# The last two attention units and the delta-rule scan: which goes first in each turn, and how the decay steps are spread

## The reference

```python
h = rmsnorm(x, norm1_w); proj = h @ w_in
o_a = gated_delta_rule(qa, ka, va, g, beta)          # 4 heads, chunks of 64 tokens
o_a = rmsnorm(o_a, gdn_norm_w) * silu(z)
o_b = dilated_attention(qb, kb, vb)                  # 8 heads of 64 features
x = x + concat([o_a, o_b]) @ w_out
...
def step(state, xs):                                 # inside gated_delta_rule, 8 chunks in sequence
    u = uv - wk @ state
    o = qd @ state + at @ u
    state = ge * state + ke.T @ u
```

## Time and profile before

| | us |
|---|---|
| median of 3 timed runs (1449.32 to 1449.98) | 1449.7 |
| the profiled execution | 1449.33 |
| its span, first to last instruction | 1447.5 |
| TensorE busy | 1419.6 (98%) |
| VectorE busy | 817.4 (56%) |
| ScalarE busy | 610.7 (42%) |
| GpSimd busy | 134.3 (9%) |
| decays stage (panels 141 to 143) | about 906.8 to 935 |
| panel 147 with scan and units 10 and 11 | 978.5 to 1026.5 |

### The profile page before, as it was taken

The page is one execution under the profiler, slowest core; times in us unless marked ns, Lnnn a source line. Parts: engine busy times, 40 slices in busy tenths (PEclk is TensorE's granted clock), DMA queues, the critical chain, the costliest instruction groups (busy, mean ns, idle before and its releaser), DMA issues.

```text
span 1447.5 us, 19982 instructions
## 1 busy us (share of the span) xinstructions
PE 1419.6 (98%) x7898; PEld 1134.1 (78%) x7898; DVE 817.4 (56%) x1394; ACT 610.7 (42%) x1104; POOL 134.3 (9%) x116
## 2 busy tenths in 40 slices
PE   8999999999999999999999999999999999999997
PEld 6777777788788888888877777776778888888886
DVE  4545555557674343443468767676555763664463
ACT  4544455542363231322335755344444432342234
POOL 0000000012200000000012000440020210110012
PEclk9999999999999999999999999999999999999999
DMA  7222222113223223222233221110222232222221
GB/s 254 83 82 85 87 81 73 59 59 131 88 74 116 87 102 103 87 102 89 101 106 131 88 73 59 64 42 1 103 103 85 105 106 99 90 100 102 85 66 68
DMA packets 40348, 130.92 MB, mean 90 GB/s; under 512 B 4800, under 2 KB 5184, under 8 KB 40256
## 3 DMA queue, kind: packets, MB, share of 16 engines
q1 hardware_dynamic: 39392, 128.08, 25.5%
q10 hardware_dynamic: 864, 1.57, 0.3%
HBM read 124.92 MB, written 4.19 MB: 89 GB/s over the span
## 4 chain that ended last, share of the span: by engine, by line
PE 89%; DVE 5%; ACT 3%; issue 2%; DMA 1%; POOL 0%; SPq 0%; POOLq 0%; DVEq 0%; ACTq 0%
PE bank L1254 86%; PE bank L1257 3%; ACT Fm L1637 2%; DVE Fm L2091 1%; DVE Fm L1986 1%; DVE Wlo L1986 1%; ACT Whi L1637 1%; DVE Fm L1994 1%; POOL Fm L2570 0%; DVE Xf L1986 0%; DMA Fm<-in_relb_dram 0%; DMA Fm<-in_x_dram 0%; SPq L2665 0%; DVE sm L1990 0%; POOL Xf L2570 0%
## 5 line engine op out<-in xcount | busy, mean ns | idle before, releaser
L1254 PE MATMUL bank<-Rm,Whi 128*128 128x512 f32 x2816 | 872.7, 391 | 9.0 <-ACT Whi L1637 5.7
L1254 PEld LDWEIGHTS bank<-Rm,Whi 128*128 128x128 f32 x2816 | 529.8, 188 | 120.4 <-ACT Whi L1637 5.7
L1254 PE MATMUL bank<-Rm,Wlo 128*128 128x512 f32 x1408 | 563.2, 400 | 1.5 <-issue 1.3
L1986 DVE TENSOR_TENSOR Wlo<-Wraw,Whi 128x1024 fp32r<-128x1024 f32 (+2 forms) x225 | 283.9, 1265 | 143.1 <-ACT Whi L1637 142.5
L1254 PEld LDWEIGHTS bank<-Rm,Wlo 128*128 128x128 f32 x1408 | 265.2, 188 | 62.6 <-issue 8.2
L1637 ACT ACTIVATE Whi<-Wraw 128x1024 fp32r<-128x1024 f32 (+2 forms) x225 | 232.5, 1038 | 191.8 <-PE bank L1254 186.2
L1254 PE MATMUL bank<-Xr,Whi 128*128 128x512 f32 x736 | 226.8, 389 | 0.0
L2570 POOL TENSOR_TENSOR Fm<-Fm 128x512 f32<-128x512 f32 (+1 forms) x86 | 112.8, 1320 | 775.9 <-ACT Fm L1637 483.0
L1254 PEld LDWEIGHTS bank<-Xr,Whi 128*128 128x128 f32 x736 | 138.1, 188 | 28.7
L1637 ACT ACTIVATE Fm<-bank 128x512 f32<-128x512 f32 (+4 forms) x200 | 92.6, 483 | 150.0 <-PE bank L1254 103.0
L1986 DVE TENSOR_TENSOR Fm<-Fm,bank 128x512 f32<-128x512 f32 (+2 forms) x118 | 76.0, 664 | 121.9 <-PE bank L1254 121.7
(11 more groups left out here) (100 smaller groups left out, 712.4 us busy)
## 6 DMA issues: line engine op xcount, KB each, us to landing
Wraw<-in_w_in_dram SPq DMA_DIRECT2D x67, 512.0 KB, 3.3
Wraw<-in_w_ff_dram SPq DMA_DIRECT2D x64, 512.0 KB, 3.2
Wraw<-in_w_up_dram SPq DMA_DIRECT2D x44, 512.0 KB, 3.2
Wraw<-in_w_o_dram SPq DMA_DIRECT2D x16, 512.0 KB, 3.3
Wraw<-in_w_down_dram SPq DMA_DIRECT2D x16, 512.0 KB, 3.2
Wraw<-in_w_ab_dram SPq DMA_DIRECT2D x8, 512.0 KB, 3.3
Wraw<-in_w_down_end_dram SPq DMA_DIRECT2D x8, 384.0 KB, 2.9
Fm<-in_relb_dram SPq DMA_DIRECT2D x8, 256.0 KB, 3.9
```

The lines of the kernel that those rows point to most:

```text
L1254: return e.matmul(o, l, r, start=first, stop=last)
L1986: return e.tensor_tensor(o, x, y, op)
```

## The change

The generator of the last units gives up its lone eighth step: a unit's `headout` is followed at once, in the same step, by the first step of the next unit; the last `headout` stands in the fifteenth turn. In each turn the units' step comes before the scan's. And the decay steps go 3, 3, 2 over the three panels instead of 2, 3, 3.

```diff
-STEPS_DECAYS = (2, 3, 3)
+STEPS_DECAYS = (3, 3, 2)
...
     def last_units():
-        yield from heads(10)
-        yield from heads(11)
+
+        for unit in (heads(10), heads(11)):
+            for _ in range(7):
+                next(unit)
+                yield
+            next(unit)
...
-    side.append(in_turn([gdn_scan(), last_units()]))
+    side.append(in_turn([last_units(), gdn_scan()]))
```

## The result

| | before | after |
|---|---|---|
| time, median of five runs each | 1449.7 us (1449.23 to 1453.25) | 1456.59 us (1455.72 to 1458.72) |
| profiled execution, its span | 1449.33, 1447.5 us | 1458.72, 1456.9 us |
| ratio of the times | | 1.0042, 95% interval 1.003 to 1.0054 |
| mean granted clock of the span | 0.997 | 0.993 and 0.995 |

The changed kernel is slower by 6.9 us at the medians (6.1 by the ratio). The forecast was 1450.9, with a range that ended at 1453.4: it is wrong, and on the side that was given a quarter.

What follows compares the result with a forecast made beforehand. TensorE, busy 98% of the span, was taken as the bound. Scan +2.0 (7.2 + 0.7 - 5.9, including 1.7 for the clock) and decays -0.8 gave +1.2 on 1449.7: 1450.9 us, range 1448.8 to 1453.4.

Steps and rivals of the forecast that it cites:

- the early fall: Granted clock at 1.2 GHz from about 982.7 to 986.1 us, in the scan; forecast to go, saving 1.7 us.
- Decays, -0.8: Decays stage: second `inv0` stops waiting for GpSimd, -1.0; second `decay1` waits for bank 7, +0.2; bounds -1.0 and 0.
- neither hide nor give back: Claim that stages behind the changed ones leave their gains and losses intact, read from TensorE's gaps in ten-microsecond windows.
- R4: Rival: decays bring nothing, because another input of the second `inv0` ends with GpSimd's; 1451.7 us, chance 0.05.
- The walk through the scan: Engines followed item by item in the new order: waits 7.2 us, transposes' switching 0.7, against 4.2 of old waits.
- R3: Rival: the new waits in the middle of the scan are hidden; 2.0 us less, 1448.9 us, chance 0.12.
- R1: Rival: a late fall of the clock at 1022 to 1026 us, costing 1.7, so 1452.6 us; chance 0.27.
- a second half-clock stretch there: Sign that the prediction is wrong: a half-clock stretch at the end of the scan, around `scan1` 8.
- since dense products follow at once: Reason for pricing a fall at the scan's end at 1.7 us, the same as the fall at 982.7.
- The argument against R1: TensorE's wait of 1.69 us at 1005.74, in the scan, had passed without a fall of the clock.
- both falls and the far ends: Cases outside the range 1448.8 to 1453.4; early and late clock falls together meant 1454.3 us, chance 0.03.
- The sum's own range: Range given to the summed total of 1450.9 us, before the rivals: 1450.0 to 1452.0 us.

Runs made afterwards that it cites:

- e4: Changed kernel with three products of constants between `scan2` 7 and `scan1` 8, written to a bank nobody reads: 1452.87 us, ratio 1.0018.
- e1: Kernel before with only the decay steps changed to 3, 3, 2: 1450.96 us, ratio 1.0007.
- e3: Changed kernel with `headout` 11 moved back behind `scan1` 8: 1451.62 us, ratio 1.0006.
- e2: Changed kernel with the old decay steps 2, 3, 3, so the new scan order alone: 1458.08 us, ratio 1.0057.
- e11: Changed kernel with one product of constants between `scan2` 7 and `scan1` 8: 1454.52 us, ratio 1.0029.
- e8: Kernel before with only `headout` 11 moved ahead of `scan2` 7: 1455.28 us, ratio 1.0028.
- e5: Kernel before with only `headout` 10 moved one step later, behind `scan2` 4: 1449.89 us, ratio 0.9996.

## Why the prediction was wrong, point by point

The three differences that the account rests on: the order without a fall, +4.1 to +4.2; the decays, -0.7; the late fall, 3.5 at the ratios. Sum: 4.1 - 0.7 + 3.5 = 6.9 us, against 6.9 at the medians and 6.1 by the ratio. That it meets the medians to a tenth is luck, since it adds stages of single traces to a difference of ratios: the order with its gap filled (e4) is 3.4 above the kernel before by the stages, and 2.6 by the ratio, with 1.2 to 3.9 as its interval. The forecast had 3.7 - 0.8 - 1.7 = 1.2. Both terms of the clock failed, and they carry 5.2 of the 5.7 us. So the step that failed is the clock: the late fall, put at nothing in the sum and at 1.7 us as a rival, cost 3.5, and the early fall, credited at 1.7 in full, was no fixed part of the time before.

- *Decays, -0.8.* Right in the trace: the wait of 0.97 is gone, GpSimd's chain ends with 1.25 us to spare (1.9 by the forecast), and the stage is 0.69 shorter in all traces with 3, 3, 2. The sentence that the stages behind "neither hide nor give back" stays open for it. From panel 144 to 147 the traces with 3, 3, 2 have 43.4 us on average and the ones with 2, 3, 3 43.0, but each set spreads by about 1 us, so the 0.4 isn't settled; e1's time shows no gain. R4's mechanism, another input that ends with GpSimd's, is refuted by the missing wait; whether its sum was right hangs on those 0.4 us.
- *The walk through the scan: 7.2 + 0.7 of new cost against 4.2 of old waits, +3.7.* Measured +4.1 to +4.2, near. `scan1` 8 was 2.5 and is 2.53, `scan1` 4 1.0 and 1.00, `scan1` 9 0.6 and 0.58, `value` 2 0.8 and 0.67, `scan2` 2 0.3 and 0.25, `scan2` 0 0.4 and 0.31; `scan1` 6 was 0.3 and is 0.49. The brackets of the timeline sum to 5.8, which is only 1.6 more than the 4.2 of before. The rest isn't drawn as idle: the sixteen products at 986.31 take 2.69 us where eight like them took 0.90, about 0.9 too long, and some 1.6 us are placed by no row; the forecast had 0.7 for changes of form, which nothing here tests by itself. So the end of the walk is confirmed item by item, and its middle by the total alone. R3, the middle hidden, is refuted: e3, which has only the middle and the front, is 2.2 longer than e1, 0.7 of it the gap that it keeps at `scan1` 8.
- *The clock, what goes: 1.7.* Credited in full, because the profiled execution of before had the fall. e1 had the same items there and none (46.53 for 48.04, so 1.5 is what it costs where it comes). The kernel before was timed at mean clocks from 0.995 to 0.999. The traces without any fall but the one that ends each of them have 0.998 or 0.999, those with one more of 3.4 us 0.997; 25 of the 80 runs of the kernel before are at 0.998 or 0.999, so most likely without it. The median to which I added the difference was therefore not one with that fall in every run, and a fall seen once should have been a chance in the sum, not a term.
- *The clock, what comes: R1.* The place is right, give or take a microsecond (1026.6 for 1022 to 1026), and the gap is its cause, as e3 and e4 show; a second half-clock stretch there was the forecast's own sign of being wrong. Price and chance are wrong. The price was taken from the only fall in sight, 3.4 us long, "since dense products follow at once"; but `scan1` 8, 0.58 us of idle and `scan1` 9 follow first, and the stretch became 6.8 us in e2 and 10.2 in the profiled execution of after. Whether this thin work made it longer wasn't tested, and it can't be all, since both kernels have the same items there. Its cost, from stages: after 52.87 - 50.76 = 2.1 in the scan and 1.85 in the 76 products behind, 4.0 us; e2 1.1 + 1.6 = 2.7. The chance was 0.27; it is in both profiled executions with the gap of 2.53, and all ten runs of the two kernels have a mean granted clock of 0.993 to 0.995, where e4's ten are at 0.997 to 0.999. A fall of 10.2 us in 1457 takes 0.0035 off that mean, so the eight that were not profiled most likely had it too, though the mean doesn't say where a fall stands: 10 of the 80 runs of the kernel before are at 0.995 as well. With price 3.5 and nothing credited for the early fall, the same walk would have given 1449.7 + 3.7 - 0.8 + 3.5 = 1456.1.
- *The argument against R1*, that 1.69 us at 1005.74 passed without a fall, was weaker than it looked: by these traces that wait stands among products that run in pairs, behind which 28 more follow at once, and the one before `scan1` 8 has four half-used products ahead of it and a second gap behind.
- *The rule of the Trainium skill* ("TensorE: Matmul & The Clock Gate", section "HAM oscillation — how this bites in real kernels"), which lays the falls on long gaps without any matmul, gave no fall at either place. The runs don't agree with it at the gaps of this kernel: 2.53 us went with a late fall in both profiled executions that had it, and e4, where the gap is filled, has none. Setting the rule aside was right; what it was replaced by was too weak.
- *The range.* It left out "both falls and the far ends". R1 at the price measured, 3.5 us over the 1450.9, lies outside it. The length of one fall, seen once, was taken as if it were the cost. The sum's own range was too narrow too: new waits of 3.5 to 8.2 us and decays of -1.0 to 0 give about 1447 to 1452.7, not 1450.0 to 1452.0.

What stays open: what decides from one execution to the next whether the clock falls early in the scan, at 753.6 or in the tail, and whether a fall lasts 3.4, 6.8 or 10.2 us; some 1.6 us of the middle of the scan; and the 0.4 us behind the decays.

## What to carry to other kernels

An item whose result nobody needs soon can still stand in the way of one that is needed at once. Before moving it, read the in-order queue of each engine that it uses: here the output's low part, which waits for ScalarE, stood ahead of the states, which TensorE waited for. Where a reorder opens a gap of TensorE of 2 us among small products, count the clock as well as the gap, give its price a range of more than the one fall in sight, and take a fall that one trace shows as a chance.

## What the runs showed of the hardware

- A longer gap of TensorE among the same small products, ahead of the same `scan1` 8, went with a lower clock: 0.70 us (e3) and 1.47 (e11) no fall in the profiled executions, and mean clocks of 0.996 to 0.999 in the runs compared; 1.93 (e8) a fall of 10.2 us in the profiled one, and 0.992 to 0.998 in seven runs; 2.53 (after, e2) falls in both profiled ones, and 0.993 to 0.995 in all ten runs.
- The stretches at 1.2 GHz, apart from the one that ends each trace, measured 3.4, 6.8 or 10.2 us. One of 3.4 us cost 1.5 us in the scan (before against e1), 0.8 among the panel products at 753.6 (after) and 1.1 to 1.7 in the tail. At the lower level `scan1` 8's 20 products took 3.02 us for 1.67.
- Falls also came and went where the items are the same: near 983 between before, e5 and e8 (3.4 us, none and 6.8), at 753.6 and in the tail between before and after. A stage that nobody touched can therefore differ by 1.5 us or more between two traces. The stretch ahead of panel 141 differs by 2.6 us (906.81 in before, 909.43 in e5) with no fall in either.
- Products of constants in a gap can pay. In e4 they returned 3.5 us, although `scan1` 8 comes no earlier (47.4 us behind the first product of panel 147, for 47.2 in after).
